# V rows gathered by token and summed with a 32-column coefficient stripe, in place of V rows gathered by slot and summed with diagonals

## The chip, the core and the metric

The kernel runs on 1 core of one Trainium2 chip. The time is that of the device in microseconds (us), taken as the median of several runs: before, 3569.66 us over 3 runs (3557.79 to 3579.22). Engines: PE (TensorE), DVE (VectorE), ACT (ScalarE), POOL (GpSimd), SP (SyncE, which issues plain DMAs). POOL issues the indirect DMAs.

## The reference

One step of a layer over 1024 prompt tokens (plus 16 meta tokens) and 32 sample tokens, of width 1024, all in float32. First comes a mixer (projections, a short convolution, a gated recurrence, an mLSTM in chunks), then PEER, which is what the change touches:

```
qh = (xb @ wq).reshape(128, 8, 2, 128)           # a block of 128 tokens, 8 heads
s1, s2 = qh[:, :, 0] @ keys1.T, qh[:, :, 1] @ keys2.T
v1, i1 = top_k(s1, 16);  v2, i2 = top_k(s2, 16)
sc, ci = top_k(v1[:, None] + v2[None, :], 16)    # of 256 sums
e    = i1[ci // 16] * 128 + i2[ci % 16]          # one of 16384 experts
gate = softmax(sc)
act  = gelu(einsum('td,thkd->thk', xb, u_tab[e])) * gate
out  = einsum('thk,thkd->td', act, v_tab[e])
```

So each token has 8 x 16 = 128 experts (its slots). For each, a row of 1024 numbers of `peer_u` is multiplied with the token (a dot), and a row of `peer_v`, times a coefficient, is added to the token's result. That is 128 x 128 rows of each table for a block of 128 tokens, 4 KB a row.

## The kernel before

**Tokens and blocks.** The 32 sample tokens and the 16 meta tokens come first, then 8 blocks of 128 prompt tokens (`BLOCKS`), tokens on the 128 partitions. The first seven run in a hardware loop whose body ends with the first 16 slots of the next block.

**Gathers.** POOL's `gathers` (L387 to L405) issues one indirect DMA per slot and table: 128 rows of 4 KB, one for each token, picked by a column of `idx`. They go into `ring`, a ring of 8 row tiles, each 128 x 1024. A gather waits until the one that had its tile 8 places earlier has been used: `s_dot` for a U row, `s_vsum` for a V row. The order is written out by hand (`side_by_side`, `over`): U of slot t, V of slot t - 16, U of slot t + 1 and so on. For the last 16 V slots of a block the U slots are those of the next block, so U and V alternate up to the block's last 16 V gathers of all.

**Dots.** DVE's `dot` (L1259) multiplies a U row tile with `xcur` (the block's normed tokens, copied by ACT's `take_over`) and sums along the row: one column of `dots`. After each 16 slots `gelu_arg` and `coefficients`, with an exponential on ACT between them, make 16 columns of `coef`.

**Sums.** ACT's `diagonal` makes a 128 x 128 diagonal matrix from a column of `coef` (4 buffers, `diag`). PE's `expert_sum` (L684) multiplies it with the V row tile: two matmuls of 512 columns, all 128 tokens at once, added up in `acc` in PSUM, which `take_up` had filled with `h`. When all 128 are in, ACT's `finish` squares and copies `acc`, and DVE's `finish` scales it; SP stores it.

**What stands beside.** Each engine's program is a list by ticks. A tick has one dot, one V sum, and parts of two other jobs (`beside`): `query`, heads 1 to 7 of this block's top-k search and head 0 of the next one's, each some 9 small DVE steps of which most are chained, and `mixer` of the next block, from tick 30 to 109. SP reloads the query weights (`load_wq`) as PE uses them up. Nothing is reordered: what stands behind a waiting instruction on an engine waits too.

## Time and profile before

| | before |
|---|---|
| timed runs, median (3) | 3569.66 us |
| timed runs, lowest and highest | 3557.79, 3579.22 us |
| profiled execution, span | 3605.3 us |
| PE, DVE, POOL, ACT busy | 84%, 65%, 64%, 18% |
| mean granted clock of PE | 0.959 |
| moved by DMA | 1213.76 MB, mean 337 GB/s |
| packets of the gathers' queue | 304128, 1107.43 MB, 83.1% of 16 engines' span |

The profile is of one execution, a separate one from the three timed runs; the page gives its span from the first to the last instruction and no other time of it, and this span is 1.0% above the median. Busy is the union of an engine's instructions. A wait is idle time before an instruction, with what ended it: "issue" is time in which the engine waited for nothing that the profile shows, "remote" is a releaser the profile does not know. Each fp32 matmul of the program has two records on PE, one for each of two passes.

Where the time is, by the trace: from the start to 311 us sample and meta tokens and the first mixer; then eight stretches that start with a copy to `xcur`, at 311.26, 719.97, 1124.62, 1537.13 and so on up to 3178.72; the last goes on to 3605.3.

### The profile page before, as it was taken

The numbers are of one execution on the slowest core, as the hardware profiler recorded it, in microseconds if no ns is written. First come the engines' busy times: TensorE is split into PE (matmuls) and PEld (weight loads), VectorE is DVE, ScalarE is ACT, GpSimd is POOL, SyncE is SP. The second block draws the span as 40 slices with busy tenths as digits, with TensorE's granted clock in tenths as the row PEclk, the third lists the DMA queues.
The fourth block names the chain that finished last, engine by engine and source line by source line (L and its number), as shares of the span: only waits on it lengthen the run. The fifth ranks groups of instructions, "written<-read, shape, count | busy, mean of one in ns | idle before, by whom it ended". The sixth has DMA issues, their size and how long they took to land.

```text
span 3605.3 us, 39214 instructions
## 1 busy us (share of the span) xinstructions
PE 3011.3 (84%) x10724; PEld 1568.6 (44%) x10724; DVE 2354.0 (65%) x5813; ACT 658.5 (18%) x2015; POOL 2298.7 (64%) x2132
## 2 busy tenths in 40 slices
PE   7687888889987898879987798879987799877677
PEld 2553454345533454345533454345533454344222
DVE  3565975578656875578756876568655876568442
ACT  2211221112211221112211221112211121111111
POOL 0224666766777566766676567667676567667775
PEclk9799999989999999999999999999998999999999
DMA  6456989999999999999999999999999999999998
GB/s 241 161 174 240 366 316 346 371 354 351 337 372 378 348 338 351 348 361 359 330 368 357 363 314 355 361 340 369 341 353 355 364 327 345 350 375 373 355 368 296
DMA packets 340167, 1213.76 MB, mean 337 GB/s; under 512 B 41072, under 2 KB 41200, under 8 KB 339904
## 3 DMA queue, kind: packets, MB, share of 16 engines
q0 software_dynamic: 304128, 1107.43, 83.1%
q1 hardware_dynamic: 35776, 103.32, 7.7%
q8 instruction: 104, 1.70, 0.2%
q14 instruction: 159, 1.30, 0.1%
HBM read 1205.73 MB, written 4.87 MB: 336 GB/s over the span
## 4 chain that ended last, share of the span: by engine, by line
PE 37%; issue 20%; DMA 16%; DVE 9%; POOL 9%; another core or an unknown queue 6%; ACT 3%; POOLq 0%; ACTq 0%; SPq 0%; DVEq 0%
PE acc L428 23%; PE bank L428 13%; DMA ring<-peer_v,idx 11%; POOL ring L404 9%; DMA ring<-peer_u,idx 6%; DVE ring L1266 2%; ACT xn L750 1%; ACT diag L750 1%; DVE kw L1050 1%; DVE xn L1161 0%; DVE xn L1164 0%; ACT h L750 0%; ACT xT L750 0%; DVE topi L1052 0%
## 5 line engine op out<-in xcount | busy, mean ns | idle before, releaser
L428 PE MATMUL acc<-ring,diag 128*128 128x512 f32 (+1 forms) x4224 | 2086.7, 623 | 449.9 <-DMA ring<-peer_v,idx 269.1
L1266 DVE SCALAR_TENSOR_TENSOR ring<-ring,xcur 128x1024 f32<-128x1024 f32 x1056 | 1289.0, 1225 | 818.0 <-DMA ring<-peer_u,idx 744.5
L404 POOL DMA_INDIRECT ring<-peer_v,idx x1056 | 1151.2, 1090 | 643.6 <-issue 291.9
L404 POOL DMA_INDIRECT ring<-peer_u,idx x1056 | 1143.7, 1083 | 642.7 <-issue 316.5
L428 PEld LDWEIGHTS acc<-ring,diag 128*128 128x128 f32 (+1 forms) x4224 | 746.4, 192 | 1427.7 <-issue 1107.3
L750 ACT ACTIVATE diag<-ident,coef 128x128 f32<-128x128 f32 x1024 | 366.7, 395 | 646.7 <-PE acc L428 392.6
L428 PEld LDWEIGHTS bank<-xT,win 128*128 128x128 f32 (+1 forms) x2304 | 272.9, 183 | 79.2 <-issue 73.5
L428 PE MATMUL bank<-xT,win 128*128 128x128 f32 (+1 forms) x2304 | 282.6, 277 | 2.4 <-ACT xT L750 2.4
L750 ACT ACTIVATE G<-bank 128x128 f32<-128x128 f32 (+1 forms) x137 | 40.6, 296 | 830.4 <-PE bank L428 449.4
L428 PE MATMUL bank<-win,xT 128*128 128x512 f32 (+3 forms) x368 | 166.2, 583 | 1.9 <-ACT xT L750 1.9
L428 PEld LDWEIGHTS bank<-xT,qk 128*128 128x128 f32 x1024 | 131.5, 201 | 37.1 <-issue 37.1
L428 PEld LDWEIGHTS bank<-xT,t 128*128 128x128 f32 x1024 | 130.8, 200 | 36.2 <-issue 36.2
L428 PE MATMUL bank<-xT,qk 128*128 128x128 f32 x1024 | 131.3, 284 | 0.0
L428 PE MATMUL bank<-xT,t 128*128 128x128 f32 x1024 | 130.4, 283 | 0.0
L428 PEld LDWEIGHTS bank<-keysT,G 128*128 128x128 f32 x256 | 47.8, 200 | 132.9 <-issue 72.1
L428 PE MATMUL bank<-keysT,G 128*128 128x128 f32 x256 | 55.7, 301 | 57.5 <-ACT G L750 42.4
L428 PEld LDWEIGHTS bank<-win,xT 128*128 128x128 f32 (+2 forms) x368 | 60.3, 170 | 89.0 <-issue 88.7
L1266 DVE DVE_READ_ACCUMULATOR ring<-ring,xcur 128x1 f32 x1056 | 86.7, 82 | 0.0
L428 PE MATMUL bank<-wout,G 128*128 128x512 f32 (+1 forms) x144 | 70.5, 620 | 1.0 <-issue 1.0
L750 ACT ACTIVATE gl_a<-gl_a 128x16 f32<-128x16 f32 x66 | 14.0, 212 | 301.5 <-DVE gl_a L1275 154.3
L428 PE MATMUL bank<-wout,xc 128*128 128x512 f32 (+1 forms) x144 | 67.0, 593 | 0.0
L1049 DVE MAX8 tops<-bank 128x8 f32<-128x128 f32 x128 | 37.9, 296 | 31.3 <-PE bank L428 24.7
(227 smaller groups left out, 1821.1 us busy)
## 6 DMA issues: line engine op xcount, KB each, us to landing
qk<-wq SPq DMA_DIRECT2D x64, 512.0 KB
t<-wq SPq DMA_DIRECT2D x64, 512.0 KB
ring<-peer_u,idx POOLq DMA_INDIRECT x1056
ring<-peer_v,idx POOLq DMA_INDIRECT x1056
win<-w_in SPq DMA_DIRECT2D x6, 2048.0 KB, 15.1
ring<-wq SPq DMA_DIRECT2D x16, 512.0 KB, 5.1
wout<-w_out SPq DMA_DIRECT2D x1, 4096.0 KB, 22.8
xn<-x_prompt SPq DMA_DIRECT2D x8, 512.0 KB
```

What stands on the lines that cost most here:

```text
L404: pool.indirect_dma_start(out=ring[:, slot, :], out_offset=None, in_=(peer_u, peer_v)[which], in_offset=bass.IndirectOffsetOnAxis(ap=idx[: ...
L428: return nc.tensor.matmul(out, lhsT, rhs, start=start, stop=stop)
L750: return nc.scalar.activation(out, in_, func, **kw)
L1049: link(dve.max(out_v[:, 0:8], values))
L1050: link(dve.match_replace(work, out_v[:, 0:8], values, -3.0e38))
L1266: stt(row, row, 1.0, xcur[:, :], ALU.mult, ALU.mult, accum_out=dots[:, column(b, e):column(b, e) + 1]).then_inc(s_dot, 1)
```

## The change

A V gather no longer takes slot j of 128 tokens but the 128 slots of one token, so slots lie on partitions. For this the block's table `idx` (tokens x slots) is turned: copied to float, transposed by PE, copied by ACT, and made whole numbers again by DVE (`float_idx`, `turn_idx`, `turned_idx`). `coef` is turned once a block in the same way (`turn_coef`, `turned_coef`). A token's sum is then one column of coefficients against the row tile. It stands in `wz`, 128 x 32 stripes of zeros with one column set: a window of 32 columns is slid over it so that the column falls on the token's place among 32. Tokens are taken in the order 0, 32, 64, 96, 1, 33 and so on; the left half of a token's sum goes to its own 32 partitions of `acc` and the right half 64 partitions further. `take_up` and `finish` swap the right half's partitions at the start and at the end.

V rows of a block can start only when all 128 of its slots have a coefficient. So the V rows of block b - 1 run beside the U rows of block b, 8 ticks later (`LAG`), and block 0's gathers from slot 16 on and block 7's V rows have none of the other kind beside them. The coefficients are made for 64 slots at a time (`HALF`). Heads 1 to 7 of the search start 8 ticks earlier. `h` is kept in `hcur`; the norm row comes from a matmul with `ffn8` instead of a 128 x 1024 tile.

```diff
-DIAGS = 4
+SETS = 4
+GROUPS = 4
+LAG = 8
+HALF = 64
...
-T_QUERY = 1
+T_QUERY = 1 - LAG
...
+        def token_of(i):
+
+            return SAMPLE * (i % GROUPS) + i // GROUPS
...
+                    if which == V and e == 0 and b is not None:
+                        pool.wait_ge(s_idxv, b + 1)
...
+                    if which == V and b is not None:
+                        at = idxv[:, token_of(e):token_of(e) + 1]
...
+            def period(b, last):
+
+                both = [x for t in range(LAG, P) for x in ((U, b, t), (V, last, t - LAG))]
+                return [(U, b, t) for t in range(LAG)] + both + [(V, last, i) for i in range(P - LAG, P)]
...
+            gathers(first + over() + [(U, 0, t) for t in range(TOPK, P)], None)
+            with pool.Fori(1, BLOCKS - 1) as b:
+                gathers(period(b, b - 1), before_period(b))
             b = BLOCKS - 1
-            gathers(side_by_side(b, range(TOPK, P)) + [(V, b, j) for j in range(P - TOPK, P)], over(b)[-RING:])
+            gathers(period(b, b - 1) + [(V, b, i) for i in range(P)], before_period(b))
...
-            def expert_sum(b, j):
-
-                n = n_experts(b)
-                slot, arrived = row_of(1, b, j)
...
+            def token_sum(b, i):
+
+                m, g = divmod(i, GROUPS)
+                slot, arrived = row_of(1, b, i)
+                if g == 0:
+                    pe.wait_ge(s_wz, sets_before(b) + m + 1)
                 pe.wait_ge(s_row[slot], arrived)
-                pe.wait_ge(s_diag, experts_before(b) + j + 1)
+                at = P * (m % SETS) + SAMPLE * (g + 1) - 1 - m
                 for half in range(2):
-                    last = mm(acc[0:n, 512 * half:512 * half + 512], diag[:, j % DIAGS, 0:n],
-                              ring[:, slot, 512 * half:512 * half + 512], start=False, stop=j == n - 1)
+                    to = SAMPLE * ((g + GROUPS // 2 * half) % GROUPS)
+                    last = mm(acc[to:to + SAMPLE, 512 * half:512 * half + 512], wz[:, at:at + SAMPLE],
+                              ring[:, slot, 512 * half:512 * half + 512], start=False, stop=m == P // GROUPS - 1)
                 last.then_inc(s_vsum, 1)
...
+            def close(b, last, more):
+
+                for k in range(LAG):
+                    if last is not None:
+                        token_sum(last, P - LAG + k)
+                    if more:
+                        queries(b + 1, k - LAG)
+                    if k == LAG - 2:
+                        turn_coef(b, more)
+                take_up(b)
...
+            def token_weights(b, m):
...
+                act.wait_ge(s_vsum, experts_before(b) + GROUPS * (m - SETS + 1))
+                to = wz[:, P * (m % SETS):P * (m % SETS) + P].rearrange("p (g c) -> p g c", g=GROUPS)[:, :, SAMPLE - 1]
+                a(to, coefT[:, :].rearrange("p (g m) -> p g m", g=GROUPS)[:, :, m], ACT.Copy).then_inc(s_wz, 1)
...
+                    a(y[:, 0:512], acc[:, 0:512], ACT.Copy)
+                    for to, of in ((0, 64), (64, 0)):
+                        last = a(y[to:to + 64, 512:1024], acc[of:of + 64, 512:1024], ACT.Copy)
+                    link(last)
+                link(a(acc[0:n, :], y, ACT.Square, accum_out=stat[0:n, 6:7]))
...
+            def turned_idx(b):
+
+                dve.wait_ge(s_itf, b + 1)
+                if not is_count(b, 0):
+                    dve.wait_ge(s_vsum, experts_before(b))
+                dve.tensor_copy(idxv[:, :], idxf[:, :]).then_inc(s_idxv, 1)
...
+            def close(b, last, more):
+                gelu_arg(b, 1)
+                for k in range(LAG):
+                    if k == 1:
+                        coefficients(b, 1)
+                    if more:
+                        queries(b + 1, k - LAG)
+                if last is not None:
+                    finish(last)
+                turned_idx(b)
```

Three places show how the order changes. On PE, in the loop, where the mixer's key projection stands; before, with one V sum (two matmuls `acc<-ring,diag`) a tick between blocks of eight projections:

```order
L428 MATMUL acc<-ring,diag 128x512 x2
L428 MATMUL bank<-xT,win 128x128 x8
L689 REGISTER_ALU
L428 MATMUL acc<-ring,diag 128x512 x2
L689 REGISTER_ALU
L428 MATMUL acc<-ring,diag 128x512 x2
L428 MATMUL bank<-xT,win 128x128 x8
```

and now, where `wz` is the stripe and the two register instructions come once in four tokens:

```order
L469 MATMUL bank<-xT,win 128x128 x8
L757 REGISTER_ALU
L758 REGISTER_ALU
L469 MATMUL acc<-ring,wz 32x512 x4
L469 MATMUL bank<-xT,win 128x128 x8
L469 MATMUL acc<-ring,wz 32x512 x4
```

The number of matmuls is the same, their place beside the mixer's too; their output has 32 rows instead of 128.

On POOL, the last gathers of the program before, at the end of block 7:

```order
L404 DMA ring<-peer_u,idx 128x1024 [waits s_dot]
L404 DMA ring<-peer_v,idx 128x1024 [waits s_vsum]
L404 DMA ring<-peer_v,idx 128x1024 [waits s_dot]
L404 DMA ring<-peer_v,idx 128x1024 [waits s_vsum]
L404 DMA ring<-peer_v,idx 128x1024 [waits s_dot]
L404 DMA ring<-peer_v,idx 128x1024 [waits s_vsum] x9
```

and now, where `s_idxv` is the turned table of block 7:

```order
L437 DMA ring<-peer_u,idx 128x1024 [waits s_dot]
L437 DMA ring<-peer_v,idxv 128x1024 [waits s_vsum]
L437 DMA ring<-peer_v,idxv 128x1024 [waits s_dot]
L437 DMA ring<-peer_v,idxv 128x1024 [waits s_vsum]
L437 DMA ring<-peer_v,idxv 128x1024 [waits s_idxv,s_vsum]
L437 DMA ring<-peer_v,idxv 128x1024 [waits s_vsum] x127
```

16 V gathers without U gathers have become 8 of block 6 and then 128 of block 7.

On DVE, the end of the loop's body before: the score search of head 1 of the next block, then `finish` (L1297), then the loop's branch and the coefficients of the last 16 slots:

```order
L1052 MAX_INDEX topi<-tops,bank 128x8 [waits s_dve]
L1053 MAX_INDEX topi<-tops,kw 128x8
L1297 SCALAR_TENSOR_TENSOR xn<-xn,stat,final_bc 128x1024 [waits s_rstd_y,s_dve]
L1336 REGISTER_ALU
L1336 COMPARE_AND_BRANCH
```

and now, with the top-16 of head 1 ahead of it and the turned table behind it; the next dot is the first after the branch:

```order
L1207 MAX_INDEX ci<-gate,kw 128x8
L1231 TENSOR_SCALAR gmax<-gate 128x1 [waits s_dve]
L1459 SCALAR_TENSOR_TENSOR xn<-xn,stat,final_bc 128x1024 [waits s_rstd_y]
L1470 REGISTER_ALU [waits s_itf]
L1471 CAST idxv<-idxf 128x128 [waits s_vsum]
L1542 REGISTER_ALU
L1542 COMPARE_AND_BRANCH
```

Before, `finish` at this place belonged to the block whose dots had ended 16 ticks earlier; now it belongs to the block before the one whose dots have just ended, and no dot of the next block stands ahead of it.

## Rows read from the trace of the kernel before

**Rows 1.** the page: span, and busy time of each engine.
```profile
span 3605.3 us, 39214 instructions
...
PE 3011.3 (84%) x10724; PEld 1568.6 (44%) x10724; DVE 2354.0 (65%) x5813; ACT 658.5 (18%) x2015; POOL 2298.7 (64%) x2132
```

**Rows 2.** windows (busy us, instructions): block 0, block 2, and block 7 to the end.
```profile
core 0: us, PE busy (x) PEld busy (x) DVE busy (x) ACT busy (x) POOL busy (x), PEclk, DMA share, GB/s
312.00:720.00 408.00, 349.00 (x1248) 179.20 (x1248) 280.15 (x685) 74.26 (x235) 275.38 (x259) 0.97 0.95 352
...
1124.60:1537.10 412.50, 351.80 (x1252) 188.08 (x1252) 281.39 (x688) 76.27 (x234) 278.42 (x257) 0.97 0.94 349
3178.70:3605.30 426.60, 315.81 (x836) 134.33 (x836) 232.54 (x584) 66.17 (x192) 295.42 (x269) 0.98 0.94 352
```

**Rows 3.** groups of instructions in block 2: busy us, mean ns, idle before, releasers.
```profile
L428 PE MATMUL acc<-ring,diag 128*128 128x512 f32 x512 | 252.6, 624 | 49.8 <-DMA ring<-peer_v,idx 29.6 <-ACT diag L750 13.5 <-issue 6.6
L1266 DVE SCALAR_TENSOR_TENSOR ring<-ring,xcur 128x1024 f32<-128x1024 f32 x128 | 156.4, 1226 | 95.0 <-DMA ring<-peer_u,idx 87.3 <-issue 6.2
L404 POOL DMA_INDIRECT ring<-peer_v,idx x129 | 139.7, 1083 | 83.1 <-issue 33.5 <-PE acc L428 20.6 <-remote 17.1
L404 POOL DMA_INDIRECT ring<-peer_u,idx x128 | 139.5, 1090 | 51.4 <-issue 40.4 <-PE acc L428 9.5 <-DVE ring L1266 1.5
```

**Rows 4.** waits of POOL in block 2: us in total, times, longest.
```profile
POOL ring L404 <- PE acc L428: 30.2, 29, 7.1
POOL ring L404 <- remote: 17.1, 7, 2.9
POOL ring L404 <- DVE ring L1266: 13.4, 7, 2.2
```

**Rows 5.** timeline of POOL around the longest of these waits.
```profile
1178.35 0.94 POOL L404 DMA_INDIRECT ring<-peer_u,idx  x1 [7.08 <-PE acc L428]
1179.59 0.94 POOL L404 DMA_INDIRECT ring<-peer_v,idx  x1 [0.30 <-issue]
```

**Rows 6.** waits of DVE in block 2: the first and last not on gathers.
```profile
DVE gl_a L1283 <- issue: 7.7, 2, 4.0
...
DVE xc L1121 <- ACT xl L750: 0.7, 1, 0.7
```

**Rows 7.** block 2 in eight windows: two of them.
```profile
1227.70:1279.30 51.60, 43.06 (x191) 26.02 (x190) 43.38 (x129) 13.45 (x42) 35.55 (x34) 1.00 0.95 353
1279.30:1330.90 51.60, 50.41 (x252) 31.92 (x251) 39.26 (x74) 13.24 (x42) 36.23 (x33) 1.00 0.94 338
```

**Rows 8.** groups in 3300 to 3500, block 7 without mixer: U gathers, V gathers.
```profile
L404 POOL DMA_INDIRECT ring<-peer_u,idx x69 | 78.5, 1137 | 22.4 <-issue 16.7 <-PE acc L428 5.5 <-remote 0.3
L404 POOL DMA_INDIRECT ring<-peer_v,idx x68 | 74.5, 1095 | 25.6 <-issue 16.4 <-PE acc L428 7.0 <-remote 1.5
```

**Rows 9.** timeline of PE: last sums, and two 32-column sums of the sample.
```profile
3570.42 27.70 PE L428 MATMUL acc<-ring,diag 128*128 128x512 f32 x64 [0.22 <-issue]
...
239.51 1.90 PE L428 MATMUL acc<-ring,diag 128*32 128x512 f32 x4
241.34 3.70 PE L428 MATMUL bank<-win,xT 128*128 128x512 f32 x8
```

**Rows 10.** windows of 0.5 us in the sample queries, 32-column matmuls on PE.
```profile
106.45:106.95 0.50, 0.50 (x7) 0.50 (x6) 0.00 (x0) 0.50 (x1) 0.00 (x0) 1.00 0.00 0
107.50:108.00 0.50, 0.50 (x11) 0.50 (x9) 0.00 (x0) 0.00 (x0) 0.00 (x0) 1.00 0.99 180
```

**Rows 11.** timeline of ACT and DVE after the last sum.
```profile
3598.16 1.02 ACT L750 ACTIVATE xn<-acc 128x1024 f32<-128x1024 f32 x1 [6.46 <-PE acc L428]
...
3600.79 1.28 DVE L1297 SCALAR_TENSOR_TENSOR xn<-xn,stat,final_bc 128x1024 f32<-128x1024 f32 x1 [30.95 <-ACT stat L750]
```

**Rows 12.** timeline: the first gather of block 0 on POOL, its dot on DVE.
```profile
310.83 1.12 POOL L404 DMA_INDIRECT ring<-peer_u,idx  x1 [29.79 <-DVE idx L1084]
...
315.32 1.23 DVE L1266 SCALAR_TENSOR_TENSOR ring<-ring,xcur 128x1024 f32<-128x1024 f32 x1 [3.00 <-DMA ring<-peer_u,idx]
```

More of the change, by code:

```diff
@@ L270, in looped @@
         def looped(v):
-            return not isinstance(v, int)
+            return not isinstance(v, int) or v > 2
         block = ctx.enter_context(nc.Block())
@@ L641, in query @@
                         pe.wait_ge(s_topk, heads_before(b) + head - 1)
+                    if ft == 5 and not is_count(b, 0):
+                        pe.wait_ge(s_ct, b)
                     pe.wait_ge(s_q2, b * 16 + ft + 1)
@@ L701, in beside, with period @@
                     query(b + 1, 0, tick - T_QUERY0)
+                if tick == T_IDX:
+                    turn_idx(b)
+            def period(b, last, more):
+                for tick in range(P):
+                    if tick >= LAG:
+                        token_sum(last, tick - LAG)
+                    beside(b, tick, more)
+            def close(b, last, more):
[7 more added lines that the diff above has]
+                take_up(b)
             for tick in range(T_MIXER, BLOCK_TICKS):
@@ L1287, in dots_of @@
-            def dots_of(b, e):
-                dot(b, e)
+                width = TOPK if b is None else HALF
+                heads = width // TOPK
+                first = column(b, width * g)
+                d, c, x = dots[:, first:first + width], coef[:, first:first + width], gl_a[:, 0:width]
+                dve.wait_ge(s_dot, experts_before(b) + width * (g + 1))
+                link(tt(x, d, d, ALU.mult))
+                link(ts(x, x, GELU_CUBIC, 1.0, ALU.mult, ALU.add))
+                link(tt(x, x, d, ALU.mult))
```

373 lines of the change are left out of this document (232 added, 141 removed).

## The prediction

> **What bounds the kernel now.** I read the busy shares first, then windows by block, then POOL's groups and waits, since POOL issues every gather. PE is busy 84%, DVE 65%, POOL 64% [rows 1]: no engine is full over the whole span. A block between two copies to `xcur` takes (3178.7 - 720.0)/6 = 409.8 us in the loop, with PE 352, DVE 281 and POOL 278 us busy, and the DMA engines at 0.94 to 0.95 [rows 2]. POOL's busy time leaves out the time between two gathers: one that waits for nothing starts 0.30 us after the last [rows 5]. In block 2 a gather takes (139.7 + 139.5)/257 = 1.086 us on POOL [rows 3], so 256 of them need 256 x 1.386 = 355 us, and 57 us of the 412.5 are POOL's waits for a ring slot. Of these PE's sums name 30.2, rows with a releaser "remote" (unknown) 17.1, and dots 13.4 [rows 4]. The longest wait, 7.08 us, is at the gather of expert 16, once a block [rows 5]. So the bound is POOL's pace, with PE taking most of what is lost above it: in the stretch of the mixer's projections PE is busy 50.4 of 51.6 us while the DMA rate falls to 338 GB/s [rows 7]. DVE comes third: 43.4 of 51.6 us in another stretch [rows 7].
>
> **PE, removed and added.** A V row costs four records now (two halves, each fp32 matmul shown as two); at the end 64 of them run in 27.70 us, 0.433 each, 1.73 us a row, 222 us a block [rows 9]. The change still has four, with 32 columns. Width alone saves nothing: the sample's 32-column sum takes 1.83 us until the next starts [rows 9]. What can save is that the two halves now write different 32-partition groups. The trace has one place where that happens, the sample's query tiles, four groups of 32 partitions: inside one group 7 records fall into 0.5 us, where it passes from one group to the next 11 do [rows 10]. Two groups ran at once, at nearly twice the rate. I take 2 x 0.433 = 0.87 us a row; no gain, 1.73, is the other end. A change of width costs about 1.83 - 1.73 = 0.10 us [rows 9], two a row, so 1.06 us where other work stands beside the row: 0.67 x 128 = 86 us less PE a block.
>
> The Trainium skill bears on this twice. "TensorEngine Tiling (Array Packing)", key properties: tiles run matmuls and weight loads in parallel, but changing the mode drains the engine. The row agrees that a change costs something, 0.10 us. "TensorE: Matmul & The Clock Gate", part 3, gives 2.38 times for three column tiles; its efficiency of 0.79 would make a row about 1.1 us instead of 0.87, an estimate from that page, and would take some 20 to 30 us of the 86 away. Both leave PE well below the period.
>
> **ACT and DVE, removed and added.** ACT loses 128 diagonals a block and gets 32 copies of four columns and a copy of h; PE's wait for diagonals, 13.5 us a block [rows 3], becomes one wait in four rows, for copies made four sets ahead. DVE works on 64 columns twice instead of 16 columns eight times; some 50 small instructions go, about 7 us. The index table, its two transposes and the norm row through PE add some 4 us to PE and 1 to DVE; hidden, as PE has over 100 us free.
>
> **The period after.** The waits that go: PE's 30.2 and most of "remote", 47.3 less 36 starts of 0.30 = 36.5; I let 27 go, since DVE is next (the dots' 13.4 stay, and where DVE is at 43 of 51.6 it becomes the pace). The 7.08 us wait goes with these. Added: at a block's end eight V gathers stand alone, then eight U gathers. Dot 0 stands on DVE behind `finish` of the block before, which waits for its last sum, then ACT's new chain (three copies, a square, two small ones: about 4 us; now 2.6), then 1.28 us [rows 11]. U8 waits for that dot: last landing + about 1 + 4 + 1.3 + 0.3 + 1.3 = 8, where POOL is ready some 4 to 5 us after that landing. 3 to 5 us, taken as 5. Period: 409.8 - 27 + 5 = 388. Its ends: 355 (POOL never waits) and 415 (nothing gained, the boundary paid).
>
> **What is added once.** V rows of a block can start only when all its coefficients exist, so they run in the next block's period. Block 0's gathers of U from 16 on stand alone, and after block 7's period 128 V gathers stand alone. The sum:
> - to the `xcur` copy of block 0: 311.3, unchanged (the first gather of block 0 starts at 310.8 [rows 12]).
> - block 0 to dot 0 of block 1: DVE-bound. Its work 280 [rows 2] - 7, its waits for other things than gathers 28 (twelve groups, 7.7 down to 0.7, in block 2 [rows 6]), close 7: 308. The DMA queues half idle here; the same block took 408 before, with its V rows. Ends: 290, 335.
> - six periods: 6 x 388 = 2328.
> - block 7's period and the V rows of block 7: 376 gathers are left after U7. Without mixer POOL needs (78.5 + 74.5)/137 + 0.30 = 1.417 us for one and waits only 48.0 - 41.1 = 7 us in 200 [rows 8]: 533. Boundary 3.
> - a stall before the first V row of block 7: its table is written by DVE behind `finish` of block 6, 7 us after the last landing; POOL would go on at once, some 4.5 to 6 us before that landing (a gather issued at 310.83 is used at 315.32 in an empty queue [rows 12]). 13.
> - the end: landing 6, sum 1, ACT 4, DVE 1.3, and from DVE's end at 3602.1 to the span's end 3.2 [rows 1, 11]: 16.
>
> 311.3 + 308 + 2328 + 533 + 3 + 13 + 16 = 3512 us against 3605.3, -2.6%. Split: block 0 gains 100, six periods 131, and everything behind costs 3512 - 2947 = 565 where it took 426.6 [rows 2], 138 lost. The three timed runs have a median of 3569.66, 0.990 of the profiled span; so 3512 x 0.990 = 3477, I say 3478. The extra structure costs 38 us net of its own; the gain hangs on the period: the break-even is 388 + 93/6 = 403.5.
>
> **Rivals.**
> 1. The two halves do not run at once, so the change doesn't do what it says on PE. For it: the evidence is a passage of eleven records. Against: it is the same kind of matmul. Period 415, and 128 V rows alone at 1.73 instead of 1.417, +40: 3512 + 162 + 40 = 3714, or 3677. Slower.
> 2. DVE takes the place of PE. Queries and dots in the first 36 ticks want 3 us a tick, dot 0 starts late and DVE never catches up; the waits on PE become waits on dots. For it: DVE at 43 of 51.6 us, and 13.4 us of waits on dots already. Against: over the whole block DVE has 120 us free. If next to nothing of a period is gained, it is 407 to 412, with 408 taken: 3512 + 120 = 3632, or 3596, slower; it decides from 403.5 on. Its milder half, 401 to 406, ends within half a per cent of before.
> 3. More goes than I think: PE's relief and the lost boundary wait bring POOL near its floor. Period 372: 3512 - 96 = 3416, or 3382. For it: 355 is the floor. Against: DVE's dense stretch.
> 4. A token's 128 rows lie elsewhere in HBM than 128 tokens' rows of one slot; the rate of V gathers may change either way. Nothing in the trace tells. 5% of the V half is 9 us a period, 60 in all. It widens the range.
>
> **Chances.** What a measurement of this kernel can tell from no change is about 0.5% (3552 to 3587). Forecast, period 377 to 400, 0.50; rival 3, 0.11; rival 2's mild half, 0.13; its other half 0.16; rival 1, 0.07; slower by rival 4 or by something else, 0.03. Faster 0.61, same 0.13, slower 0.26. The forecast's own range is 3412 to 3548; for 8 in 10, 3390 to 3620.
>
> **What would show it.** Right: four records of a token's sum inside about 1.1 us, PE busy near 250 us a block; a loop period of 380 to 395 us with POOL's waits named after dots and not after sums; block 0 with DVE over 85% busy and about half the DMA rate; a gap of some 13 us on POOL, then 128 V gathers at 1.4 us. Wrong: a sum of 1.7 us (rival 1); waits on dots over 35 us a period (rival 2); V gathers that take POOL or the queues longer than U gathers (rival 4); or a mean of POOL's gather far from 1.09 us, on which the whole sum rests.

## The result

The changed kernel takes 3660.78 us (median of 4 runs, 3660.55 to 3661.57), the kernel before 3571.01 us on the same chip (4 runs, 3557.79 to 3579.22): ratio 1.025, 95% interval 1.021 to 1.029. It is slower by 2.5%, where 2.6% faster was forecast (3478 us), and its time lies above the range. PE's busy time went down (2616 us in place of 3011), and the kernel still lost.

The two traces do not show the whole loss. The one of the kernel before is of an execution of 3605.3 us, 1.0% above the median of its timed runs; the one of the changed kernel is of an execution at its median. So the spans lie 54.5 us apart and the medians 90. An estimate for the kernel before at its median takes 1.0% off each of its parts: 406 us in place of 409.7 for a period.

First the page of the changed kernel, which answers to [rows 1], with its granted clock in 40 slices:

```profile
span 3659.8 us, 37362 instructions
...
PE 2616.4 (71%) x10900; PEld 1097.5 (30%) x10900; DVE 2286.7 (62%) x5425; ACT 365.3 (10%) x1239; POOL 2303.3 (63%) x2131
...
PEclk9798777788788977798778976798778987755599
```

The mean granted clock is 0.802, before it was 0.959. Next the windows from one copy to `xcur` to the next, as in [rows 2]: block 0, block 3, and block 7 to the end.

```profile
core 0: us, PE busy (x) PEld busy (x) DVE busy (x) ACT busy (x) POOL busy (x), PEclk, DMA share, GB/s
316.90:614.20 297.30, 168.26 (x834) 115.96 (x833) 269.48 (x645) 38.32 (x120) 184.38 (x149) 0.76 0.83 291
1414.70:1826.10 411.40, 304.20 (x1276) 129.69 (x1272) 273.55 (x640) 39.91 (x139) 282.16 (x257) 0.81 0.95 350
3054.80:3659.80 605.00, 408.02 (x1323) 82.36 (x1323) 226.54 (x532) 31.75 (x121) 399.21 (x387) 0.74 0.94 352
```

Block 0 is short and DVE is busy 91% of it, as forecast. A block in the loop is about as long as before (2 us longer, if the period before is put at 406), though PE works 48 us less in it. The end is long. In the parts of the forecast's sum, with dot 0 of a block as the mark:

| us, in the profiled executions | before | forecast | after |
|---|---|---|---|
| start to dot 0 of block 1 | 722.2 | 619 | 626.0 |
| six periods | 2458.4 | 2328 (6 x 388) | 2449.6 (6 x 408.3) |
| dot 0 of block 7 to the end | 424.7 | 565 | 584.2 |
| span | 3605.3 | 3512 | 3659.8 |

Of the 148 us between forecast and result in spans, 122 stand in the six periods, 19 behind them, 7 ahead. Between the timed medians it is 183: the forecast took 1.0% off its sum, since the kernel before had been profiled in an execution so much slower than its median, and the changed kernel's profiled execution was not. That is 35 us more, which no part of the kernel caused. The largest part is the period, so the question is one period. Its groups in block 3, to be held against [rows 3] (the V gathers are those of block 2):

```profile
L469 PE MATMUL acc<-ring,wz 128*32 128x512 f32 x516 | 165.4, 756 | 90.8 <-DMA ring<-peer_v,idxv 80.8 <-issue 9.8
L1419 DVE SCALAR_TENSOR_TENSOR ring<-ring,xcur 128x1024 f32<-128x1024 f32 x128 | 156.0, 1225 | 100.6 <-DMA ring<-peer_u,idx 82.9 <-issue 16.4
L437 POOL DMA_INDIRECT ring<-peer_v,idxv x129 | 149.0, 1155 | 61.3 <-issue 37.5 <-DVE ring L1419 9.7 <-PE acc L469 9.5
L437 POOL DMA_INDIRECT ring<-peer_u,idx x128 | 134.1, 1047 | 68.3 <-issue 38.3 <-DVE ring L1419 16.3 <-PE acc L469 11.8
```

PE's sums are busy 165.4 us in place of 252.6. (A record's mean of 756 ns counts overlapping records each in full.) POOL's mean gather is (149.0 + 134.1)/257 = 1.10 us, nearly what it was. POOL's waits by releaser in the same stretch, as in [rows 4]:

```profile
POOL ring L437 <- issue: 75.8, 222, 2.0
POOL ring L437 <- DVE ring L1419: 26.0, 10, 8.6
POOL ring L437 <- PE acc L469: 21.4, 22, 3.9
POOL ring L437 <- remote: 6.4, 3, 2.4
```

Waits on PE and "remote" fell from 47.3 to 27.8 us, those on dots rose from 13.4 to 26.0. I add up, period by period, what POOL idles above 0.30 us ahead of each gather that waits over 0.60: before, 48 to 58 us in blocks 2 to 6, 53.7 on average, of which 3.4 stand at the first 20 gathers of a period and one wait of about 7 at the gather of expert 16 [rows 5]. After, 51.5 us on average, but 28.5 of it stand at the first 20 gathers of a period and 23.0 at the other 236. About half of the waits in the middle of a block did go; as much came back at its boundary.

The 28.5 us divide into three parts, means of blocks 2 to 6: 6.5 at the gathers U0 to U7, 8.7 at U8, 13.3 at the eleven behind it.

The trace shows a cause for each. First PE at the end of block 3, rows of the timeline:

```profile
1828.58 2.05 PE L469 MATMUL bank<-xT,qk 128*128 128x128 f32 x16
1830.56 1.05 PE L469 MATMUL acc<-ring,wz 128*32 128x512 f32 x4
1836.24 0.80 PE L469 MATMUL bank<-keysT,G 128*128 128x128 f32 x2 [4.63 <-ACT G L854]
1836.97 1.92 PE L469 MATMUL acc<-ring,wz 128*32 128x512 f32 x4
...
1846.33 1.05 PE L469 MATMUL acc<-ring,wz 128*32 128x512 f32 x4
```

The last V sums are mixed with head 1's query of the next block. Its key product waits 4.6 us for ACT's copy of the query, and the V sums stand behind it in PE's order; the last of them runs at 1846.33. The copy itself is short and late:

```profile
1835.91 0.28 ACT L854 ACTIVATE G<-bank 128x128 f32<-128x128 f32 x1 [8.81 <-remote]
```

It waits for nothing but the query's own matmuls on PE, and comes 5.3 us after the end that the first row above gives them (at the end of block 4 it comes 0.04 us after it). The ends of PE's records are modelled, so the time may be PE's own; what kept this copy waiting is not shown. (At 1830.56 the four records take 1.05 us, at 1836.97, at half clock by the trace, 1.92.) POOL, whose U gathers need the slots of these sums:

```profile
1832.69 0.94 POOL L437 DMA_INDIRECT ring<-peer_u,idx  x1 [2.04 <-issue]
...
1836.82 0.94 POOL L437 DMA_INDIRECT ring<-peer_u,idx  x1 [1.95 <-remote]
1839.79 0.94 POOL L437 DMA_INDIRECT ring<-peer_u,idx  x1 [2.03 <-PE acc L469]
1843.79 0.94 POOL L437 DMA_INDIRECT ring<-peer_u,idx  x1 [3.07 <-PE acc L469]
...
1857.92 1.09 POOL L437 DMA_INDIRECT ring<-peer_u,idx  x1 [8.69 <-DVE ring L1419]
1860.72 0.94 POOL L437 DMA_INDIRECT ring<-peer_v,idxv  x1 [1.72 <-DVE ring L1419]
```

Then the chain that ends in dot 0, first ACT's copies of `acc`, then DVE:

```profile
1847.43 1.80 ACT L854 ACTIVATE xn<-acc 128x512 f32<-128x512 f32 x3 [0.66 <-PE acc L469]
```

```profile
1851.18 1.28 DVE L1459 SCALAR_TENSOR_TENSOR xn<-xn,stat,final_bc 128x1024 f32<-128x1024 f32 x1 [2.90 <-ACT stat L854]
1852.39 0.22 DVE L1471 CAST idxv<-idxf 128x128 uint32<-128x128 f32 x1
1855.88 1.22 DVE L1419 SCALAR_TENSOR_TENSOR ring<-ring,xcur 128x1024 f32<-128x1024 f32 x1 [3.27 <-issue]
...
1858.68 1.22 DVE L1419 SCALAR_TENSOR_TENSOR ring<-ring,xcur 128x1024 f32<-128x1024 f32 x1
```

Dot 0 waits for nothing but the loop's branch: 3.27 us of "issue". (2.1 to 4.6 us in blocks 2 to 6, and 0.0 in block 7, which stands behind the loop. The kernel before has such a wait too, 4.0 us at L1283 in block 2 [rows 6], but not ahead of dot 0.) Eight gathers wait in the ring by then, and dots follow at 2.6 to 2.9 us, with DVE steps of heads 1 and 2 between them, so POOL waits about 2 us for each of its next gathers.

### The profile page after: what moved, and what is told of

Same layout as the page of the kernel before. It is cut to its first block, busy times and chain, and to the rows that moved or that the text cites. A ratio compares the mean times of both kernels' runs of the same rounds, so it can differ in the third digit from the quotient of the medians.

```text
span 3659.8 us, 37362 instructions
## 1 busy us (share of the span) xinstructions
PE 2616.4 (71%) x10900; PEld 1097.5 (30%) x10900; DVE 2286.7 (62%) x5425; ACT 365.3 (10%) x1239; POOL 2303.3 (63%) x2131
## 4 chain that ended last, share of the span: by engine, by line
issue 27%; DMA 20%; DVE 19%; PE 16%; POOL 11%; another core or an unknown queue 4%; ACT 2%; POOLq 1%; DVEq 0%; SPq 0%; ACTq 0%
DMA ring<-peer_v,idxv 13%; POOL ring L437 11%; PE acc L469 8%; PE bank L469 8%; DVE ring L1419 8%; DMA ring<-peer_u,idx 7%; DVE kw L1204 1%; DVE eh L1215 1%; DVE kw L1214 1%; DVE kw L1212 1%; DVE topi L1206 1%; ACT xn L854 1%; DVE xn L1312 1%; DVE tops L1205 1%
## 5 line engine op out<-in xcount | busy, mean ns | idle before, releaser
L469 PE MATMUL acc<-ring,wz 128*32 128x512 f32 x4224 | 1400.6, 753 | 714.4 <-DMA ring<-peer_v,idxv 620.6
L437 POOL DMA_INDIRECT ring<-peer_u,idx x1056 | 1123.5, 1064 | 792.7 <-issue 466.4
L437 POOL DMA_INDIRECT ring<-peer_v,idxv x1024 | 1144.3, 1117 | 513.2 <-issue 281.0
L469 PEld LDWEIGHTS acc<-ring,wz 128*32 128x32 f32 x4224 | 175.1, 119 | 1574.5 <-DMA ring<-peer_v,idxv 1225.6
L469 PE MATMUL bank<-xT,win 128*128 128x128 f32 (+1 forms) x2304 | 312.5, 295 | 7.1 <-issue 4.7
L469 PE MATMUL bank<-win,xT 128*128 128x512 f32 (+3 forms) x368 | 185.6, 640 | 1.9 <-ACT xT L854 1.9
L469 PEld LDWEIGHTS bank<-xT,qk 128*128 128x128 f32 x1024 | 157.0, 242 | 88.0 <-issue 86.4
L469 PE MATMUL bank<-xT,qk 128*128 128x128 f32 x1024 | 169.0, 332 | 19.0 <-DMA qk<-wq 15.4
L469 PE MATMUL bank<-xT,t 128*128 128x128 f32 x1024 | 148.6, 305 | 17.3 <-issue 12.5
L854 ACT ACTIVATE wz<-coefT 128x4 f32<-128x4 f32 x256 | 49.6, 206 | 451.4 <-PE acc L469 294.4
```

The source lines that it names most:

```text
L437: pool.indirect_dma_start(out=ring[:, slot, :], out_offset=None, in_=(peer_u, peer_v)[which], in_offset=bass.IndirectOffsetOnAxis(ap=at, a ...
L469: return nc.tensor.matmul(out, lhsT, rhs, start=start, stop=stop)
L854: return nc.scalar.activation(out, in_, func, **kw)
```

## The experiments

All are edits of the changed kernel unless they say otherwise. Ratios are to the kernel before, run beside them on one chip each time. "Period" is (dot 0 of block 7 - dot 0 of block 1)/6 in the profiled run; "first 20" and "others" are POOL's waits above 0.30 us a period, means of blocks 2 to 6, as above; "behind" is from dot 0 of block 7 to the end. Each of these four comes from one profiled execution: the two of the changed kernel differ by 1.9 us in the period and 4.1 in "others", the two of run 8's kernel by 0.9 and 0.6.

| run | ratio (interval) | clock | period | first 20 | others | behind |
|---|---|---|---|---|---|---|
| changed kernel | 1.025 (1.021-1.029) | 0.802 | 408.3 | 28.5 | 23.0 | 584.2 |
| 1 same group | 1.026 (1.021-1.031) | 0.942 | 414.4 | 28.0 | 31.1 | 586.9 |
| 2 query late | 0.999 (0.997-1.001) | 0.819 | 398.8 | 10.1 | 29.3 | 587.0 |
| 3 finish late | 1.017 (1.012-1.022) | 0.808 | 408.7 | 25.1 | 26.0 | 585.4 |
| 4 both late | 1.000 (0.998-1.002) | 0.827 | 398.5 | 11.6 | 30.1 | 582.8 |
| 5 changed kernel again | 1.021 (1.017-1.026) | 0.805 | 410.2 | 28.0 | 27.1 | 584.4 |
| 6 plain rows | 1.019 (1.015-1.024) | 0.809 | 410.2 | 26.7 | 23.7 | 583.8 |
| 7 wide sums | 1.036 (1.032-1.041) | 0.942 | 412.7 | 28.2 | 29.0 | 626.1 |
| 8 take_up late | 0.995 (0.993-0.998) | 0.824 | 395.4 | 9.0 | 29.6 | 579.6 |
| 9 as 8, wide sums | 1.008 (1.005-1.010) | 0.950 | 398.1 | 11.0 | 34.4 | 621.1 |
| 10 as 8, half rows | 0.976 (0.972-0.980) | 0.819 | 386.5 | 5.8 | 11.4 | 574.4 |
| 11 before, half rows | 0.983 (0.979-0.987) | 0.961 | 401.1 | | | 425.9 |
| 12 changed, half rows | 1.011 (1.007-1.016) | 0.803 | 406.1 | 27.3 | 10.4 | 587.3 |
| 13 as 8 again | 0.995 (0.992-0.998) | 0.825 | 396.3 | 9.6 | 30.2 | 575.7 |
| 14 as 8, filler in 1 of 4 | 0.998 (0.995-1.001) | 0.865 | 398.1 | 9.6 | 32.0 | 587.6 |
| 15 as 8, filler in 1 of 2 | 1.007 (1.004-1.010) | 0.903 | 402.3 | 9.9 | 35.9 | 592.9 |
| 16 changed, filler in 1 of 2 | 1.029 (1.024-1.033) | 0.885 | 417.1 | 27.4 | 37.0 | 591.5 |

**1. Both halves in one group of 32 partitions.** In the sums, and so in `take_up` and the two `finish`:

```diff
-                    to = SAMPLE * ((g + GROUPS // 2 * half) % GROUPS)
+                    to = SAMPLE * g
```

> The changed kernel (3661 us) with both halves of a token's sum in the same 32 partitions, so that the two halves of a sum can't run at once; nothing else moves. Theory A (the block boundary: three things in a row hold POOL back some 28 us a period, PE's sums matter little elsewhere): PE takes 1.73 to 1.83 us a sum, the waits on sums come back, some 20 us a period and 40 us in the stage with V rows alone: 3800 us, 3760 to 3840. Theory B (PE's lower clock, 0.81 after against 0.97 before, eats what the overlap gives): the clock comes back to 0.95 or more with the longer sums, and the time stays within 1% of 3661.

Ratio 1.026 and clock 0.942: the time came out as theory B had it and the clock nearly (0.95 or more), and theory A's 3800 us failed. But the edit does not remove the overlap altogether: tokens in a row still go to different groups, and records of two tokens run at once. A row of PE's timeline in the last stage:

```profile
3597.50 9.17 PE L469 MATMUL acc<-ring,wz 128*32 128x512 f32 x26
```

That is 0.353 us a record, 1.41 a row, against 0.433 and 1.73 [rows 9]. So the run says little by itself; run 7 was made for what it missed.

**2. Head 1's search back to tick 1.** No query step stands between the last V sums any more:

```diff
-T_QUERY = 1 - LAG
+T_QUERY = 1
...
+                    if more:
+                        act.wait_ge(s_xcur, streams_before(b) + 2)
```

(The wait keeps ACT's `finish` from writing `xn` before the copy to `xcur` is made.)

> The changed kernel with the search of heads 1 to 7 back at its old ticks (T_QUERY = 1), so that no query step stands between the last eight V sums of a block on PE, nor ahead of the norm on DVE. Theory A (boundary): the last V sums no longer wait behind a query matmul that waits for ACT and weights; POOL's waits in the first 20 gathers of a period, 28 us now, fall to about 18, and DVE has only dots in the first tick: 3661 - 7 x 8 = 3600, 3570 to 3625. Theory B (clock) and theory C (DVE's whole work sets the period, wherever its steps stand): no change, 3645 to 3680.

Ratio 0.999: nearly the whole loss is gone with this one number, more than the boundary theory had expected. POOL at the end of block 3 and the first row of DVE's chain:

```profile
1803.07 0.94 POOL L437 DMA_INDIRECT ring<-peer_u,idx  x1 [2.01 <-PE acc L469]
...
1811.78 0.95 POOL L437 DMA_INDIRECT ring<-peer_u,idx  x1 [0.30 <-issue]
1819.66 1.14 POOL L437 DMA_INDIRECT ring<-peer_u,idx  x1 [6.93 <-DVE ring L1421]
1821.11 1.99 POOL L437 DMA_INDIRECT ring<-peer_v,idxv  x1 [0.30 <-issue]
```

```profile
1817.62 1.23 DVE L1421 SCALAR_TENSOR_TENSOR ring<-ring,xcur 128x1024 f32<-128x1024 f32 x1 [4.45 <-issue]
```

Before U1 to U7 one wait of 2 us is left here, behind U8 none, and the one on dot 0 remains, 6.9 us, the longest of its kind. On average of blocks 2 to 6 the three parts are 3.0, 4.6 and 2.5 us, where they were 6.5, 8.7 and 13.3: most of what goes stood behind U8, where DVE's steps lay between the dots, and 3.5 us stood at the gathers that wait for the last V sums. Since the edit moves head 1's steps on PE, ACT and DVE together, no run takes these apart. The period falls by 9.5 to 11.4 us (against the two runs of the changed kernel), the waits of the first 20 gathers by 18, and those of the others rise from 23.0 and 27.1 to 29.3: some of head 1's work is now in the way later.

**3. `finish` and the turned table behind dots.** On DVE alone (here and in runs 4, 8 to 10 and 13 to 15 block 1 also stands ahead of DVE's loop, which starts at block 2):

```diff
+                    if tick == 1:
+                        turned_idx(b - 1)
+                    if tick == 4 and not is_count(b, 1):
+                        finish(b - 2)
...
-                if last is not None:
-                    finish(last)
-                turned_idx(b)
+                if not more:
+                    turned_idx(b)
+                    finish(last)
```

> The changed kernel with DVE's turned table moved behind dot 1 of the next period and its finish of the block before behind dot 4 (for block 7 the table stands ahead of the finish). Theory A (boundary): dot 0 no longer waits for the last V sum, ACT's chain and finish; it starts right after head 1's steps: about 6 us a period less, and 4 to 5 us less ahead of the last V rows: 3615, 3590 to 3635. Theories B and C: no change, 3645 to 3680.

Ratio 1.017, under 1% better than the changed kernel and not clear of it; the period hardly moves. U8 waits 4.3 us in place of 8.7, but the eleven gathers behind it wait 15.5 in place of 13.3: head 1's steps still lie between the dots.

**4. Both.**

> Both moves of the last two kernels together: dots 0 and 1 of the next block stand directly behind the coefficients on DVE. Theory A (boundary): U rows are used as soon as they land, POOL's waits in the first 20 gathers of a period fall from 28 us to under 8: 7 x 20 + 5 = 145 less, 3515 us, 3480 to 3560, faster than the kernel before (3571). Theory B (clock) and theory C (DVE's whole work): at most the sum of two small effects, above 3600.

Ratio 1.000, no better than run 2 alone; the expectation (3515 us, waits of the first 20 under 8) failed. PE shows the new wait:

```profile
1809.30 1.05 PE L469 MATMUL acc<-ring,wz 128*32 128x512 f32 x4
1817.46 3.70 PE L469 MATMUL acc<-hcur,ident 128*128 128x512 f32 x6 [7.11 <-ACTq L1075]
1821.83 2.05 PE L469 MATMUL bank<-xT,qk 128*128 128x128 f32 x16 [0.67 <-issue]
```

`take_up` waits until ACT has copied `acc` out, and head 1's query stands behind it.

**5. The changed kernel again**, as a control on the chip of runs 6 to 8.

> The changed kernel once more, as it is, on the chip of the runs that follow, so that they can be set against it. Ratio to the kernel before 1.025 (1.021 to 1.029), period 408 us. Nothing is told apart by it alone.

Ratio 1.021 (1.017 to 1.026); the two intervals meet.

**6. Plain rows.**

```diff
-                nc.tensor.transpose(bF[:, 0:P], idxf[:, :], ident[:, :]).then_inc(s_it_ps, 1)
+                mm(bF[:, 0:P], ident[:, :], idxf[:, :]).then_inc(s_it_ps, 1)
```

> The table of V rows is copied through PE but not turned, so a V gather takes the rows of one slot of 128 tokens, as before the change; the sums are then of the wrong rows, which leaves the turning out of the computation and nothing else. Boundary theory (the loss stands in what is chained between the last V sum and dot 0 to 8 of the next block): no change against the changed kernel, ratio 1.025 to the kernel before, within 0.5%. Rival 4 of the prediction (128 rows of one token lie elsewhere in HBM than 128 rows of one slot, which slows V gathers): the loss goes or halves, ratio 1.00 to 1.012, and the 128 V gathers at the end take less than 1.42 us each. Third possibility: one token's rows are the faster ones, then 1.03 or more.

The order of the rows is left out, nothing else. Ratio 1.019 against run 5's 1.021: the same. Where a token's rows lie in HBM is not the cause; rival 4 falls.

**7. Wide sums.**

```diff
-                at = P * (m % SETS) + SAMPLE * (g + 1) - 1 - m
+                at = P * (m % SETS)
                 for half in range(2):
-                    to = SAMPLE * ((g + GROUPS // 2 * half) % GROUPS)
-                    last = mm(acc[to:to + SAMPLE, ...], wz[:, at:at + SAMPLE],
+                    last = mm(acc[:, ...], wz[:, at:at + P],
```

> A token's sum is made with a window of 128 columns into all 128 partitions of acc, both halves in place: no two column groups at once, no 32-column matmuls; the result adds rows of other tokens, so the placing of the sums is left out. A row should cost PE 1.73 us at full clock instead of 1.05, 87 us more a period, so PE busy about 390 of 408 us. If the overlap of the two halves is worth what the prediction said (27 us of waits a period, 1.73 against 1.42 us for each of the last 128 rows): +190 +40 us, ratio 1.08 to 1.09. If PE is off the path and the granted clock rises with its work (0.80 to over 0.9): ratio 1.025 to 1.04. The run with both halves in one group of 32 partitions came out at 1.026, but there the rows of two tokens in a row could still run at once.

The placing of the sums is left out. Ratio 1.036, +1.5% over run 5 (52 us), where 1.08 to 1.09 was expected if the overlap was worth the prediction's 27 us, and 1.025 to 1.04 if PE was off the path. A row of PE's timeline in the last stage, and PE's line of the page:

```profile
3559.42 16.04 PE L469 MATMUL acc<-ring,wz 128*128 128x512 f32 x37
```

```profile
PE 3047.3 (82%) x10884; PEld 1603.9 (43%) x10884; DVE 2290.6 (61%) x5425; ACT 365.9 (10%) x1239; POOL 2290.8 (61%) x2131
```

0.434 us a record, 1.73 a row: no overlap. PE is busy 3047 us in place of 2605, and of the 57 us by which the profiled span is longer, 42 stand behind dot 0 of block 7, where V sums run alone, and only 2.5 in each period. So what the halves' overlap gives in a period is 2.5 us, little more than the 1.9 by which the two profiled executions of the changed kernel differ. It is a net figure: the granted clock rose to 0.942 with the longer sums and gave back some of what they cost (PE is busy 353 of 413 us in place of 299, 54 more, where the sums add 87 at full clock).

**8. `take_up` late as well.** On top of run 4, on PE, with `T_HCUR` from 3 to 9:

```diff
+                    if tick == LAG:
+                        take_up(last)
...
                     if k == LAG - 2:
                         turn_coef(b, more)
-                take_up(b)
```

> As the fourth run (search of head 1 back to tick 1, finish and the turned table behind dots 1 and 4 of the next block), and besides PE fills acc with h only at tick 8, ahead of the first V sum, no longer ahead of head 1's query; ACT keeps h at tick 9. Boundary theory: in the fourth run PE waited about 7 us for the copy of acc before it could start head 1's query, and DVE 4.6 us for that; these go, 5 to 10 us a period, 35 to 70 us in all: ratio 0.98 to 0.99. Rival (DVE's dense ticks 1 to 36 set the pace, and whatever is gained at the boundary is lost there): ratio 1.00 as in the fourth run, waits after the first 20 gathers of a period rising from 29 us.

Ratio 0.995 (0.993 to 0.998), and 0.995 (0.992 to 0.998) when run again as run 13, between the 0.98 to 0.99 of the boundary theory and the rival's 1.00: faster than the changed kernel by 2.6% and than the kernel before by half a per cent. POOL's and DVE's rows at the end of block 3:

```profile
1796.05 0.94 POOL L437 DMA_INDIRECT ring<-peer_u,idx  x1 [3.38 <-PE acc L469]
...
1808.51 1.13 POOL L437 DMA_INDIRECT ring<-peer_u,idx  x1 [0.30 <-issue]
```

```profile
1800.34 1.23 DVE L1423 SCALAR_TENSOR_TENSOR ring<-ring,xcur 128x1024 f32<-128x1024 f32 x1 [10.53 <-DMA ring<-peer_u,idx]
```

Dot 0 now waits for its row and nothing else, and U8 for nothing. The waits of the first 20 gathers are 9.0 us, those of the others stay at 29.6.

**9. Wide sums in that kernel.** The edit of run 7 in the kernel of run 8.

> The kernel of the eighth run (head 1, finish, turned table and take_up late; 0.995 of the kernel before) with the 128-column sums of the seventh: a row costs PE 1.73 us again and no two column groups run at once; the placing of the sums is left out of the computation. In the changed kernel the same edit cost 53 us, 2.5 us a period and 37 us behind it. If PE's relief is worth more once the boundary no longer hides it: 8 to 15 us a period, ratio 1.02 to 1.035. If it is worth as little as there: ratio 1.01.

Ratio 1.008: 2.7 us a period against run 8 (1.9 against run 13), 41.5 behind (45.4). That PE's overlap is worth 8 to 15 us a period once the boundary is mended is not so.

**10 to 12. Half rows**, in the kernels of run 8, before and after:

```diff
-                        out=ring[:, slot, :], out_offset=None, in_=(peer_u, peer_v)[which],
+                        out=ring[:, slot, 0:cols], out_offset=None, in_=tables[which],
```

with `tables` seen as 32768 rows of 512, `cols` = 512. The index is not doubled, so what is fetched is not the left half of each row but half row e of the table seen in this way, which lies in the first half of it; run 6 shows that the order of rows does not matter, none that this does not.

> The kernel of the eighth run with gathers of 2 KB a row in place of 4 KB from block 1 on, and the right half of xcur set to nought: the right halves of all rows are left out of the computation, while every engine has the same instructions (ACT one small copy more a block). The eighth run has a period of 395 us with the DMA engines at 0.97, and 128 V gathers alone at 1.42 us each, 365 GB/s, although POOL starts one every 1.24 us where nothing is waited for. DMA theory (the rate of the queues is what holds the period above POOL's pace): 128 V gathers at 1.24 to 1.3 us, period 360 to 380, ratio 0.93 to 0.97. DVE theory (the dense ticks are all that is left): period 388 to 395, ratio 0.985 to 0.995, only the V stage shorter.

> The kernel before with the same 2 KB gathers from slot 16 of block 0 on: the right halves of all rows are left out of the computation. If PE's order of sums and projections bounds it, as the prediction had it: period 400 to 410, ratio 0.98 to 1.0. If the DMA rate does (its engines are at 0.94 to 0.95): period 370 to 390, ratio 0.90 to 0.96.

> The changed kernel with the same 2 KB gathers from block 1 on: the right halves of all rows are left out of the computation. The boundary is a chain of PE, ACT and DVE steps and not of transfers, so it should stay at 22 to 30 us of waits a period; what goes beyond it is the DMA's share. DMA theory: period 375 to 395, against 408; otherwise 403 to 408.

With half of the bytes the period falls by 8.9 us in the kernel of run 8, by 8.6 in the kernel before and by 2.2 to 4.1 in the changed one. Run 10 lies between its two expectations, run 11 in the range of PE's order and above that of the DMA rate, run 12 in the range that was not the DMA theory's. So half of the bytes is worth some 9 us a period in the kernel before and in the one with the mended boundary, and is not what tells them apart. In run 12 the others' waits fall to 10.4 us and the boundary's stay at 27.3: the boundary is a chain of engine steps, not of transfers. The last stage refutes the DMA theory's other half, V gathers at 1.24 to 1.3 us. V gathers on POOL, run 8 (3390 to 3550) and run 10 (3370 to 3490):

```profile
L437 POOL DMA_INDIRECT ring<-peer_v,idxv x111 | 104.0, 937 | 58.0 <-issue 34.9 <-PE acc L469 22.8 <-remote 0.3
```

```profile
L440 POOL DMA_INDIRECT ring<-peer_v,idxv x83 | 78.4, 944 | 43.4 <-issue 29.0 <-PE acc L472 14.1 <-remote 0.3
```

(104.0 + 58.0)/111 = 1.46 us a gather and (78.4 + 43.4)/83 = 1.47: the same, at 364 and at 179 GB/s. What holds this stage above 1.24 us (0.94 + 0.30) isn't the bytes; what it is stays open.

**13. The kernel of run 8 again**, beside the next three.

> The kernel of the eighth run once more, as it is, to confirm its 0.995 and to stand beside the next two: ratio 0.995 (0.992 to 0.998), period 395 us, clock 0.82.

**14 to 16. Filler.** Every fourth or second token's sum is done first with a stripe of zeros, in the kernel of run 8 (14, 15) and in the changed one (16); run 14 has `g == 0`:

```diff
+                if g % 2 == 0:
+                    for half in range(2):
+                        to = SAMPLE * ((g + GROUPS // 2 * half) % GROUPS)
+                        mm(acc[to:to + SAMPLE, ...], wz[:, SETS * P:SETS * P + SAMPLE],
+                           ring[:, slot, ...], start=False, stop=False)
```

> The same kernel with one token's sum in four done twice, the first time with a stripe of zeros: four records of 32x512 more in four rows, nothing in the result. PE has about 28 us more work a block at full clock. Clock theory (the granted clock falls to 0.82 because PE has gaps, and its half-clock stretches take back what the overlap gives): the clock rises to 0.87 or more, PE's own waits in the query steps shrink, and the time falls or stays, ratio 0.985 to 0.995. Rival (PE is off the path, its clock decides nothing): 0.994 to 1.000, by the 28 us of work that lie beside other waits.

> The same with every second token's sum done twice with zeros: some 56 us more PE work a block at full clock. Clock theory: clock 0.90 or more, ratio 0.985 to 1.000. Rival: 0.998 to 1.005; the wide sums, with 87 us more work a block, gave 1.008.

> The changed kernel with every second token's sum done twice with zeros. Clock theory: the boundary's PE steps (the last V sums between head 1's query steps, keysT, take_up) run at full clock, ratio 1.010 to 1.020 against 1.021 to 1.025. Rival: 1.022 to 1.032, since 37 us of the wide sums' 53 lay in the V stage at the end and half of that comes back here.

The clock rose as meant, to 0.865, 0.903 and 0.885, and no run was faster: runs 14 and 15 are slower than run 13 on the same chip (by 17 and 39 us), run 16 at 1.029 is not clear of the changed kernel's 1.021 and 1.025. The boundary's waits stay (9.6, 9.9, 27.4) and the others' are higher. That a higher granted clock would give the forecast's gain is refuted as far as a filler can tell; a higher clock without added work wasn't tried. How a filler in every second row costs 6 to 9 us a period when the wide sums cost 2.5 to 2.7 isn't explained by its work: PE is busy 312.9 of 400 us with it in run 15, and 353 of 400 in run 9.

## Why the prediction was wrong

**The failed step is "The period after"**: 388 us, made of 27 us of waits that go and 5 that the boundary adds. Measured: 408.3, which makes 122 of the 183 us by which the time was missed (35 more are the 1.0% taken off the sum). The term that was mis-sized is the boundary, 28.5 us by POOL's waits where it had 5: head 1's search, which the change moves across the boundary, was priced at nothing. The other term came out near its size, but not by the mechanism that it was given.

*The boundary, 5 us.* The prediction followed one path to dot 0: last V sum, ACT, `finish`, dot. It left out that `T_QUERY = 1 - LAG` puts head 1's search between the last V sums on PE and between the first dots on DVE. It had this edit in front of it and priced it at nothing, with no work named that hides it. Run 2 undoes that edit alone: 9.5 to 11.4 us a period and 2.2 to 2.6% of the time. The path that it did follow was about right by itself: U8 waits 4.6 us on average in run 2 where 3 to 5 were taken, though DVE's "issue" at the loop's branch ahead of dot 0, 3.9 to 4.8 us there, was not in the sum. With head 1's search in the way it is 8.7. Moving this path away gives little: `finish` alone leaves the period as it was (run 3), and with the query late it gives 0.3 us, then 2.2 to 3.1 more with `take_up` late (run 4 against runs 13 and 8), little more than two executions of one kernel differ by. By the waits the boundary costs 28.5 us a period and 9.0 when mended.

*The relief, 27 us.* The 27 held the 7 us wait of [rows 5], which did go. The other waits away from the boundary fell from some 47 to 23.0 and 27.1, and with the query back they are 29.3: with the 7 it is 24 to 31 us, the size that was forecast. That is luck as far as the reason goes. The whole period is 14.3 us shorter than before in run 8, and 13.4 in run 13 (some 4 less against the estimate of 406), and of that only 2 to 3 come from running the halves at once in 32 columns (runs 7 and 9). The prediction read "PE acc" as releaser of 30.2 us [rows 4] as if shorter sums would take it away. That PE was late there by its order and its inputs rather than by a sum's length is what this suggests; no run shows it directly. What gives the rest, the 128 diagonals that ACT doesn't make (13.5 us of PE's waits [rows 3]), the small DVE steps or the new order of V, no run took apart.

**PE's cost of a row** was right at full clock: 1.05 us for four records, 1.06 taken. The column groups do overlap, so rival 1 is out; without that the time would be 1.5% longer (run 7), not the 5.7% between rival 1's 3677 and the forecast. The Trainium skill, "TensorE: Matmul & The Clock Gate", part 3, gives 2.38 times for three column tiles, which makes 0.79 a tile. The trace agrees here: two groups give 1.73/1.05 = 1.65 times, 0.82 a group. But PE's busy time fell by 48 us a block (352 to 304), not 86, as the granted clock fell with it and a sum after idle time takes 1.92 us. "PE busy near 250" was wrong for that reason.

**ACT and DVE**: DVE's busy time went from 281.4 to 273.6 us, where 7 was said. The other additions stayed hidden, save the order in which they stand.

**What is added once**: block 0 took 297.3 us from copy to copy, with DVE at 91% and 291 GB/s, not the half rate that was to show it. Up to dot 0 of block 1 it came out at 626.0, 7 late; runs 2 and 8, without head 1's steps at the boundary, have 619.2 and 619.1 where 619 was forecast (run 13 has 623.4). (The 28 us of DVE's waits in that sum are nine groups, 7.7 down to 0.7, and not twelve; nothing hangs on it.) The stall ahead of the last V rows was right, a single row of POOL:

```profile
3462.98 0.94 POOL L437 DMA_INDIRECT ring<-peer_v,idxv  x1 [12.83 <-DVE idxv L1471]
```

12.83 against 13. The 128 gathers behind it took 181.7 us from first to last, 1.43 each, against 1.417. The 19 us too much behind dot 0 of block 7 lie ahead of this row. There 248 gathers at 1.417 and the 3 us of boundary make 354; from dot 0 to the last gather before the stall, at 3449.2, it is 373.6. POOL waits 17 us at the gathers 8 to 19 there and 15 at the later ones. But this is not simply the boundary: in runs 8 and 13 the first figure is 7 and 2, the second 22 and 23, and the stretch takes 373.8 and 370.8. What holds up the later gathers there no run took apart. The extra structure costs 63 us net (584.2 - 424.7 less 722.2 - 626.0), not 38, and still 52 in run 8.

**Rivals.** Rival 2 had the period right, 407 to 412, and waits on dots did double, 13.4 to 26.0, below the 35 that were to show it. Half of its mechanism was seen: dot 0 starts late, and for eleven gathers dots are the pace. But DVE does catch up, by gather 20, and moving head 1 back into the dense ticks 1 to 36 made the kernel faster. Its span of 3632 lacks the 19 and the 7 us; its time of 3596 lacks the 35 of the scaling besides. Rival 3 did not occur; even run 8 has 395. Rival 4 is refuted by run 6. The break-even of 403.5 was too high with the structure's cost: run 2 is level with the kernel before at 398.8, where the structure costs (587.0 - 424.7) - (722.2 - 619.2) = 59 us and six periods give 6 x 10.9 = 65.

## What to carry to other kernels

When a change moves a job "earlier by a few ticks", write down the in-order queue of each engine at the seam, and ask for each waiting step what stands behind it: a query step that waited 4.6 us held V sums, these held ring slots, and the slots held the next block's gathers, while on DVE the same head's steps spaced out the dots and cost more, 11 of the 18 us that went with run 2. A wait named after an engine is not a price of that engine's work: before paying for shorter work, lengthen it (the wide sums) and see what it costs; here 0.7 us more on each of 128 rows cost some 2 to 3 us a block where other work stood beside them, and 42 us where V rows ran alone. Work that needs a whole block's result and so runs a period later has to earn its filling and draining, here 52 to 63 us, before it gains anything.

## What the runs showed of the hardware that was not expected

- Matmuls of 32 columns overlap across instructions of different tokens too. With the filler in every second row, PE's timeline shows 12 records of 128x512 in 2.20 us, over four column groups:

```profile
3499.99 2.20 PE L469 MATMUL acc<-ring,wz 128*32 128x512 f32 x12 [0.30 <-issue]
```

That is 12 x 0.433/2.20 = 2.36 times the rate of full-width ones; the next two such rows take 2.40 and 2.33 us, 2.17 and 2.23 times.

- The granted clock fell as PE's busy time did: 0.959 to 0.802 with 3011 to 2616 us busy. The wide sums brought it back to 0.942 at 3047 us busy. Between the two levels a token's sum takes 1.05 and 1.92 us.
- POOL's gathers became longer when they moved less: the mean of a gather in a period went from 1.09 us (run 8) to 1.14 us (run 10) with half of the bytes, while its waits fell by 21 us a period. The period fell by 8.9 us only. That some of a gather's length takes the place of a wait, so that "waits that go" are not gained in full, is a reading; no run shows why they grew.
- The last stage runs at 1.46 us a V gather at 364 GB/s and at 1.47 at 179 GB/s.
- DVE's first dot after the loop's branch comes 2.1 to 4.8 us after the last instruction ahead of it (changed kernel and run 2, blocks 2 to 6), with nothing else to wait for, where U rows had long landed; dot 0 of block 7, behind the loop, comes at once (0.0). In the kernel before the first instruction behind the branch waits 4.0 us in block 2 [rows 6].
- An instruction that waits for a tile of PE's can start well after the modelled end of its records: 5.3 us at 1835.91 in the changed kernel, 0.04 us at the same place a block later.
